# A two-block transformer kernel on one core: the opening turns x's first tile as it is loaded, and the position distances move to GpSimd

## What is computed

```python
h = rms_norm(x, norm_mix_pre[i])          # x * rsqrt(mean(x*x) + eps) * gain
z = h @ w_in[i]                           # (256 x 1024) @ (1024 x columns)
c_q, c_kv, k_rope, q_c, k_c, v_c, g_a, g_b, g_c = jnp.split(z, split_points, axis=-1)
...
dist = jnp.abs(pq[..., :, None] - pw[..., None, :]).astype(jnp.float32)
s = s - slopes[None, None, :, :, None, None] * dist[:, :, None, None]
```

## Time and profile before

| what | value |
|---|---|
| time, median of 3 runs | 1905.62 us (1905.6 to 1906.89) |
| profiled execution, its span from first to last instruction | 1904.2 us (the profile gives no other time of it) |
| TensorE busy | 1868.7 us, 98% of the span |
| VectorE, ScalarE, GpSimd busy | 1107.1, 958.9, 150.4 us |
| first product of TensorE starts | 13.03 us |
| moved from memory | 330.48 MB, 174 GB/s over the span |

### The profile page before, as it was taken

The page is one execution under the profiler, slowest core; times in us unless marked ns, Lnnn a source line. Parts: engine busy times, 40 slices in busy tenths (PEclk is TensorE's granted clock), DMA queues, the critical chain, the costliest instruction groups (busy, mean ns, idle before and its releaser), DMA issues.

```text
span 1904.2 us, 26150 instructions
## 1 busy us (share of the span) xinstructions
PE 1868.7 (98%) x8988; PEld 1523.3 (80%) x8988; DVE 1107.1 (58%) x1365; ACT 958.9 (50%) x1277; POOL 150.4 (8%) x259
## 2 busy tenths in 40 slices
PE   8999999999999999999999999999999999999998
PEld 7777888887877888888788887788888888868887
DVE  6666565448676575446754456655465445575454
ACT  5664454445675464445544446644454444564443
POOL 5210010001300010000100012000011000100000
PEclk9999999999999999999999999999999999999999
DMA  6335565554524546565655554455565564526553
GB/s 225 123 119 184 179 217 190 178 183 151 166 90 166 205 164 204 193 198 177 201 190 178 179 202 141 143 195 179 182 219 170 184 198 169 195 90 197 178 178 107
DMA packets 204987, 332.72 MB, mean 175 GB/s; under 512 B 11360, under 2 KB 150240, under 8 KB 204896
## 3 DMA queue, kind: packets, MB, share of 16 engines
q1 hardware_dynamic: 200240, 319.08, 49.9%
q0 software_dynamic: 3120, 11.02, 1.7%
q10 hardware_dynamic: 1536, 1.47, 0.2%
HBM read 330.48 MB, written 1.05 MB: 174 GB/s over the span
## 4 chain that ended last, share of the span: by engine, by line
PE 88%; issue 4%; DVE 3%; ACT 3%; DMA 1%; POOL 0%; DVEq 0%; SPq 0%; POOLq 0%; ACTq 0%
PE ps L571 27%; PE ps L565 27%; PE ps L556 27%; PE ps L598 3%; ACT whi L1254 1%; PE ps L771 1%; PE ps L759 1%; PE ps L787 1%; ACT prob L1352 1%; DVE wlo L1738 1%; DMA raw<-w_in_dram 0%; DVE prob L1878 0%; DMA xs<-x_dram 0%; DVE prob L1851 0%; DVE act_lo L1744 0%
## 5 line engine op out<-in xcount | busy, mean ns | idle before, releaser
L1738 DVE TENSOR_TENSOR wlo<-raw,whi 128x2048 fp32r<-128x2048 f32 (+1 forms) x306 | 690.6, 2257 | 510.3 <-ACT whi L1254 509.8
L1254 ACT ACTIVATE whi<-raw 128x2048 fp32r<-128x2048 f32 (+1 forms) x306 | 576.9, 1885 | 422.4 <-PE ps L565 422.3
L571 PE MATMUL ps<-whi,act_hi 128*128 128x512 f32 (+2 forms) x1632 | 442.0, 392 | 5.1 <-issue 2.4
L556 PE MATMUL ps<-wlo,act_hi 128*128 128x512 f32 (+2 forms) x1632 | 438.7, 387 | 0.0
L565 PE MATMUL ps<-whi,act_lo 128*128 128x512 f32 (+2 forms) x1632 | 432.2, 386 | 1.5 <-DVE act_lo L1744 1.5
L565 PEld LDWEIGHTS ps<-whi,act_lo 128*128 128x128 f32 x1632 | 303.9, 188 | 64.4 <-DVE act_lo L1744 2.3
L556 PEld LDWEIGHTS ps<-wlo,act_hi 128*128 128x128 f32 x1632 | 302.2, 188 | 61.8 <-issue 1.1
L571 PEld LDWEIGHTS ps<-whi,act_hi 128*128 128x128 f32 x1632 | 297.5, 188 | 64.1 <-issue 2.8
L1299 ACT ACTIVATE hid<-ps,stat 128x256 f32<-128x256 f32 x132 | 62.6, 474 | 282.9 <-PE ps L598 197.4
L2320 POOL TENSOR_TENSOR stat<-stat,eps 128x1 f32<-128x1 f32 x43 | 22.4, 521 | 1471.4 <-ACT prob L1286 1471.1
L1791 DVE SCALAR_TENSOR_TENSOR hid<-ps,stat,hid 128x256 f32<-128x256 f32 x132 | 63.6, 482 | 123.7 <-ACT hid L1299 123.7
(11 more groups left out here) (217 smaller groups left out, 1611.5 us busy)
## 6 DMA issues: line engine op xcount, KB each, us to landing
raw<-ffn_w_gate_dram SPq DMA_DIRECT2D x88, 512.0 KB, 4.0
raw<-ffn_w_up_dram SPq DMA_DIRECT2D x88, 512.0 KB, 5.0
raw<-ffn_w_down_dram SPq DMA_DIRECT2D x88, 512.0 KB, 3.9
raw<-w_in_dram SPq DMA_DIRECT2D x64, 512.0 KB, 4.4
raw<-w_ffn_gate_dram SPq DMA_DIRECT2D x44, 512.0 KB, 4.0
raw<-w_ffn_up_dram SPq DMA_DIRECT2D x44, 512.0 KB, 5.0
raw<-w_ffn_down_dram SPq DMA_DIRECT2D x44, 512.0 KB, 3.9
raw<-a_w_qkv_dram SPq DMA_DIRECT2D x24, 512.0 KB, 4.5
```

The lines of the kernel that those rows point to most:

```text
L556: last = nc.tensor.matmul(o, hi, a, start=False, stop=last_pass and stop and i == len(parts) - 1)
L571: nc.tensor.matmul(o, hi, a, start=start and i == 0, stop=False)
L1254: nc.scalar.activation(whi[:, u % SLOTS, 0:words], raw[:, u % SLOTS, 0:words], ACT.Copy)\
L1738: nc.vector.tensor_tensor(wlo[:, u % SLOTS, 0:words], raw[:, u % SLOTS, 0:words], whi[:, u % SLOTS, 0:words].bitcast(F32), ALU.subtract)\
```

## The change

Seven things are done, all of them in the first microseconds, apart from the last:

1. x's first tile is transposed as it is loaded (`xs` instead of `ht`). The gain comes as a column of 8 words for each partition (`first_col`, a new input of 4 KB), and VectorE multiplies it in on the way out of PSUM into `ht`; ScalarE and VectorE then take high and low parts from `ht`.
2. The gain's row is loaded once (4 KB, one partition) instead of to all partitions, and two TensorE products of a row of ones with it spread it over 128 partitions in PSUM (`first_row`), where VectorE reads it for x's second tile.
3. The 18 transposes of the identity are gone (WARM_START = 0).
4. x's second tile is issued ahead of the splits of unit 0; `posk` is issued between the splits of units 0 and 1, on a semaphore of its own, so that GpSimd's angles wait for `posq` and `freq` alone.
5. VectorE takes the low parts of x's second tile ahead of the position work.
6. Of the position work only the six steps that split positions stay on VectorE. The eight steps of distances are twelve on GpSimd, between the load of the next gains and `inverse(1)`.
7. TensorE's first four products of units 0 and 1 wait by halves of the unit (`first_hi`, `by_halves`), in each layer; ScalarE splits units 0 and 1 of each layer in two halves. The 42 start increments of semaphores are shared between TensorE and VectorE.

```diff
-WARM_SHORT, WARM_LONG, WARM_START = 6, 3, 18
+WARM_SHORT, WARM_LONG, WARM_START = 6, 3, 0
...
 # TensorE
                 for i, (outs, hi, lo, whs, wls) in enumerate(parts):
+                    if half is not None and 2 * i == len(parts):
+                        half()
...
                 if t == 0:
-                    if ready.seam:
+                    if by_halves:
+                        pe.wait_ge(sem("first_hi"), w.at("first_hi", u + 1))
+                    elif ready.seam:
                         unit_hi_there(u)
...
-            for s in counted:
+            for s in counted[0::2]:
                 pe.sem_inc(s, BASE)
             pe.wait_ge(s_ident, 2)
             w.layer = 0
-            rows(TN_MIX, "h_ready", 0)[1](0)
-            stay_warm(WARM_START)
+            pe.wait_ge(s_in["x0"], 16)
+            for g in range(2):
+                turn(TN_MIX + g, lambda j: xs[:, 0, (4 * g + j) * P:(4 * g + j + 1) * P], 4, bank=2 + g)
+            pe.wait_ge(s_in["gain"], 16)
+            for n in range(2):
+                last = nc.tensor.matmul(ps[:, n, :], one_row, first_gain[:, n * 512:(n + 1) * 512],
+                                        start=True, stop=True)
+            last.then_inc(s_row, 1)
...
 # ScalarE
+                    in_two = halves or (w.layer is not None and UNITS1 <= u < UNITS1 + 2)
...
-            act.dma_start(gains[:, 0, :], A["gains"][0:1, :].partition_broadcast(P).rearrange("p a n -> p (a n)"))\
-                .then_inc(s_in["gain"], 16)
-            act.dma_start(posk[:, :], A["positions"][0:1, :].partition_broadcast(P).rearrange("p a n -> p (a n)")).then_inc(s_in["pos"], 16)
+            act.dma_start(first_col[:, :], A["first_col"][:, :]).then_inc(s_col, 16)
+            act.dma_start(first_gain, A["gains"][0:1, :]).then_inc(s_in["gain"], 16)
...
-            turned_rows_hi(TN_MIX, (0,))
...
-            first_split(0)
+            for g, (there, n) in enumerate(((s_turned, 1), (sem("h_ready"), w.at("h_ready", 1)))):
+                act.wait_ge(there, n)
+                nc.scalar.activation(act_hi[:, 4 * g:4 * g + 4, 0:P],
+                                     ht[:, 0, g * 512:(g + 1) * 512].rearrange("p (j c) -> p j c", j=4),
+                                     ACT.Copy).then_inc(sem("turn_hi"), 1)
             act.dma_start(xs[:, 1, :], A["x"][0, P:S, :]).then_inc(s_in["x1"], 16)
-            first_split(1)
+
+            split(1, True)
+            act.dma_start(posk[:, :], A["positions"][0:1, :].partition_broadcast(P).rearrange("p a n -> p (a n)")).then_inc(s_posk, 16)
+            split(1, True)
...
 # VectorE
-            nc.vector.tensor_tensor(ht[:, 0, :], xs[:, 0, :], gains[:, 0, :], ALU.mult).then_inc(sem("h_ready"), 1)
-            turned_rows_lo(TN_MIX, 0)
...
+            first = [ht[:, 0, g * 512:(g + 1) * 512].rearrange("p (j c) -> p j c", j=4) for g in range(2)]
+            for g, done_part in enumerate((s_turned, sem("h_ready"))):
+                dve.wait_ge(sem("turn_done"), w.at("turn_done", TN_MIX + g + 1))
+                cols = first_col[:, 4 * g:4 * g + 4].unsqueeze(2).to_broadcast([P, 4, P])
+                nc.vector.tensor_tensor(first[g], ps[:, 2 + g, :].rearrange("p (j c) -> p j c", j=4), cols, ALU.mult)\
+                    .then_inc(done_part, 1)
...
-            nc.vector.tensor_tensor(ht[:, 1, :], xs[:, 1, :], gains[:, 0, :], ALU.mult).then_inc(sem("h_ready"), 1)
+            first_row = ps[:, 0:2, :].rearrange("p b n -> p (b n)")
+            nc.vector.tensor_tensor(ht[:, 1, :], xs[:, 1, :], first_row, ALU.mult).then_inc(sem("h_ready"), 1)
+            turned_rows_lo(TN_MIX, 1)
...
-            dve.wait_ge(s_parts, n_parts[0])
-            for t in range(T):
-                parts(nc.vector.tensor_scalar(mask[:, t, :], kf[:, 0, :], posf[:, 1, t:t + 1], 4096.0,
-                                              ALU.subtract, ALU.mult))
...
-            turned_rows_lo(TN_MIX, 1)
             split(1)
...
 # GpSimd
-            pool.wait_ge(s_in["pos"], 64)
+            pool.wait_ge(s_in["pos"], 48)
...
             load_gain(1, 1)
+            pool.wait_ge(s_parts, PART_STEPS)
+            for t in range(T):
+                parts(nc.gpsimd.tensor_scalar(mask[:, t, :], kf[:, 0, :], posf[:, 1, t:t + 1], 4096.0,
+                                              ALU.subtract, ALU.mult))
+                parts(nc.gpsimd.tensor_scalar(df[:, t, :], kf[:, 1, :], posf[:, 2, t:t + 1], None, ALU.subtract))
...
+                parts(nc.gpsimd.tensor_tensor(mask[:, t, :], mask[:, t, :], df[:, t, :], ALU.subtract))
+            pool.wait_ge(s_parts, n_parts[0])
             inverse(1)
-
-            pool.wait_ge(s_parts, DISTANCE_STEPS)
```

More of the change, by code:

```diff
@@ L57 @@
 ANGLE_STEPS = 25
-PART_STEPS, DISTANCE_STEPS = 6, 14
+PART_STEPS = 6
 F32 = mybir.dt.float32
@@ L366, in two_blocks @@
         s_end_result = sem("end_result")
+        s_posk = sem("posk_in")
+        s_col = sem("first_col_in")
+        s_row = sem("first_row")
+        s_turned = sem("first_turned")
+        one_row = hid[0:1, 1, 0:P]
+        first_gain = gains[0:1, 0, :]
         blk = ctx.enter_context(nc.Block())
@@ L545, in turn_hi_there, with product @@
                 pe.wait_ge(sem("turn_hi"), w.at("turn_hi", flags[:k + 1].count("1")))
-            def product(parts, start, stop, weights_lo=None, amid=None, rows_lo=None, rows_first=False):
+            def product(parts, start, stop, weights_lo=None, amid=None, rows_lo=None, rows_first=False, half=None):
                 def by_lo_weights(last_pass):
@@ L576, in product, with unit_product @@
                 return by_lo_rows(True)
-            def unit_product(u, t, kt, parts, start, stop, ready=None):
+            def unit_product(u, t, kt, parts, start, stop, ready=None, by_halves=False):
                 ready = ready or AT_ONCE
                 if t == 0:
-                    if ready.seam:
+                    if by_halves:
+                        pe.wait_ge(sem("first_hi"), w.at("first_hi", u + 1))
+                    elif ready.seam:
                         unit_hi_there(u)
@@ L589, in unit_product @@
                                weights_lo=(lambda: unit_there(u)) if t == 0 and ready.seam else None,
-                               amid=lambda i: ready.amid(t, kt + i), rows_lo=lambda: ready.rest(t, kt), rows_first=ready.rows_first and t == 0)
+                               amid=lambda i: ready.amid(t, kt + i), rows_lo=lambda: ready.rest(t, kt), rows_first=ready.rows_first and t == 0,
+                               half=(lambda: unit_hi_there(u)) if t == 0 and by_halves else None)
             def turn(k, src, n, rows=P, bank=None):
@@ L870, in layer1 @@
                                                   act_lo[:, 4 * j + k, t * P:(t + 1) * P], [vh[:, k, :]], [vl[:, k, :]])
-                                                 for k in range(4)], j == 0, j == 1, ready if c == 0 else None)
+                                                 for k in range(4)], j == 0, j == 1, ready if c == 0 else None,
+                                                by_halves=c == 0)
                             if t == T - 1 and j == 0:
@@ L1241, in _, with split @@
             done = [0]
-            def split(n):
+            def split(n, halves=False):
                 for _ in range(n):
@@ L2128, in _, with first_lo @@
             w.layer = 0
-            dve.wait_ge(s_in["gain"], 16)
-            dve.wait_ge(s_in["x0"], 16)
-            nc.vector.tensor_tensor(ht[:, 0, :], xs[:, 0, :], gains[:, 0, :], ALU.mult).then_inc(sem("h_ready"), 1)
-            turned_rows_lo(TN_MIX, 0)
-            for u in range(2):
-                for words, there, n in ((slice(0, UW // 2), s_first_hi, u + 1),
-                                        (slice(UW // 2, UW), sem("hi"), w.at("hi", u + 1))):
-                    dve.wait_ge(there, n)
+            for s in counted[1::2]:
+                dve.sem_inc(s, BASE)
+            dve.wait_ge(s_col, 16)
+            first = [ht[:, 0, g * 512:(g + 1) * 512].rearrange("p (j c) -> p j c", j=4) for g in range(2)]
[4 more added lines that the diff above has]
+                    .then_inc(done_part, 1)
+            for g in range(2):
+                hi_n[0] += 1
+                dve.wait_ge(sem("turn_hi"), w.at("turn_hi", hi_n[0]))
+                rest(act_lo[:, 4 * g:4 * g + 4, 0:P], first[g], act_hi[:, 4 * g:4 * g + 4, 0:P])\
+                    .then_inc(sem("turn_read_v"), 1)
+            def first_lo(u):
+                for words, there in ((slice(0, UW // 2), "first_hi"), (slice(UW // 2, UW), "hi")):
+                    dve.wait_ge(sem(there), w.at(there, u + 1))
                     last = nc.vector.tensor_tensor(wlo[:, u, words], raw[:, u, words],
```

52 lines of the change are left out of this document (32 added, 20 removed).

## The result

The changed kernel takes **1918.76 us** (median of 5 runs, 1917.26 to 1920.59) against 1905.6 for the kernel before in the same comparison: ratio 1.0066, 95% interval 1.0055 to 1.0077. That is 13 us slower. The forecast was 1908.2 with 1911.6 as its upper end: the sign was right, the size missed by 10.6 us.

The account below looks back on a forecast made before the run. TensorE, 98% busy, was taken as the bound, with GpSimd's chain to `inverse(1)` close under it. Delaying `z_half(0, 1)` from 31.14 to 34.0 put unit 5 at 42.2 against 39.59: 1905.62 + 2.6 = 1908.2 us, range 1904.0 to 1911.6.

Parts of the forecast that it names:

- Change = start of `z_half(0, 1)` - 31.14 - 0.27: Opening, VectorE to TensorE: total time moves with the start of `z_half(0, 1)`, forecast at 34.0, giving +2.6 us.
- so 6.25 stays: VectorE: from the start of `z_half(0, 1)` to unit 4's low part takes 6.25 us, as before.
- I take 0.40 for the eight one-input steps and 0.62 for the four others ... 6.1 us: GpSimd's twelve distance steps ahead of `inverse(1)`: 6.1 us with 0.4 of waits, bounds 4.4 to 7.4.
- The 0.04 given to steps slower than the bound: GpSimd's distance steps: a remaining chance of 0.04 that they are slower, for a change over +3.8 us.
- an estimate of 0.38 us for one input: GpSimd's distance steps: estimates from the skill page, 0.38 us for one input and 0.55 for two, 0.4 less in all.
- rival C: TensorE ahead of unit 4: the clock falls in the 5.5 us idle, +2.3 on top of 2.6, 1910.5; chance 0.22.
- the opening as running at the 1.2 GHz level: TensorE's opening: transposes 0.21 us apart early, 0.11 at 18.70, and a slow first product group, read as a low clock.
- Part 7 ... gains nothing: ScalarE's splits in each layer: cost 0.1 us of ScalarE and gain nothing at the loop's turn.
- It costs nothing as long as x's second tile is later: TensorE's opening: the first twelve products can take 5.1 us instead of 2.7, without cost while that tile comes later.
- the upper price: TensorE's opening: the two gain products were priced at 0.45 to 0.85 us each, ending by 7.6.
- The opening's 3.3 us for TensorE: TensorE reaches tile 1's low-row products at 20.0 and unit 4 at 34.7, 3.3 us gained, spent in the wait.

Follow-up runs that it names:

- e3: The kernel before with only the twelve distance steps moved to GpSimd ahead of `inverse(1)`: 1918.88 us against 1907.12, ratio 1.0062.
- e7: The changed kernel with the distances on GpSimd in seven steps over 128x512 instead of twelve over 128x256: 1918.48 us against 1907.33 for the kernel before.
- e9: The changed kernel with 80 transposes of the identity on TensorE ahead of unit 4 in each layer: 1926.54 us against 1906.92 for the kernel before.
- e4: The changed kernel with six of the twelve distance steps, absolute value left out: 1914.09 us against 1907.12 for the kernel before.
- e5: The kernel before with only 32 unused bytes of SBUF a partition added ahead of the blocks' tiles: 1909.29 us against 1907.33, ratio 1.0014.
- e6: The kernel before with only 40 unused bytes a partition, so the blocks' tiles start at multiples of 64 bytes: 1905.33 us against 1907.33, ratio 0.9993.
- e8: e1 with 8 bytes of padding and the gains' load moved from ahead of `inverse(1)` into the angle steps: 1905.07 us against 1907.33 for the kernel before.
- e1: The changed kernel with all position work back on VectorE, ahead of the low parts of x's second tile: 1906.97 us against 1907.12 for the kernel before.

## Why the prediction was wrong

**Right: the chain and its place.** "Change = start of `z_half(0, 1)` - 31.14 - 0.27" gives 38.44 - 31.14 - 0.27 = +7.03; unit 4's first product moved by 45.12 - 38.00 = +7.12. The two are this close by luck: the formula is for unit 5, and unit 4 had 0.34 us more to spare. What makes up for it is the term "so 6.25 stays": from `z_half(0, 1)` to the low part of unit 4 it was 43.71 + 1.35 - 38.44 = 6.62 us. With the gains there, VectorE's `scaled` multiplications run between the last inverses, and two of these took longer than the 0.55 us of the earlier trace rows. The sign and the engine were read correctly from the earlier trace rows, and e3 shows that this part by itself costs as much as the whole change. Unit 4's 7.12, the clock's 1.6 and the 0.4 just named are the opening's 9.15.

**The step that failed: "I take 0.40 for the eight one-input steps and 0.62 for the four others ... 6.1 us", with 7.4 as the upper bound.** Measured in the changed kernel: 11.9 us. The four steps with a scalar per partition took 1.15 and 0.93 (one held to 2.11), the four with a constant 0.83 each, the four two-input ones 0.71 each. The error was to take a copy of 128x256 (0.41) for any one-input step. The row of a two-input step (0.737) was the nearer in kind, since it does arithmetic; even that for all twelve, 9.2 with the waits, would have been 2.7 us short, 1.0 of it the held step. With the measured 11.9 the prediction's own sum gives 34.0 + 5.8 = 39.8 for `z_half(0, 1)`, less 1.5 for angle steps that ended earlier (24.39, forecast 25.9): 38.3. The 0.04 given to steps slower than the bound was far too small for a price that no row showed. The Trainium skill (GPSIMD Engine Reference, "Elementwise — side-by-side cycle accounting") gives 1.8 cycles an element as the best case of a tight loop, from which the prediction had worked out an estimate of 0.38 us for one input. With 0.83 to 1.15 us none of these steps ran like it. The 2.6 cycles for two inputs fit better: an estimate of 0.55 us for 256 columns from that page, against 1.28 - 0.71 = 0.57 us for 256 more columns in e7.

**Right in kind, its weight mis-set: rival C.** The clock fell in the idle ahead of unit 4. It was priced at 2.3 us and cost 1.6 (e9). Since it follows from a long idle, it belonged into the sum as soon as the idle was forecast at 5.5 us: e4, with 5.86 us idle, had it too. The prediction also read the opening as running at the 1.2 GHz level. The distances of transposes and products say half rate, but the granted clock of the profile is 1.00 from 0 to 16 us in both traces, so that level is read off the distances alone. That transposes can keep the clock up is shown by e9; that the 18 had raised it is read from the one slow product alone.

**Missing: the tiles' place in SBUF.** "Part 7 ... gains nothing" and the column of gains were costed at nothing. e5 shows 1.6 to 2.0 us for 32 bytes. What remains of the 2.2 (0.1 at the turn, 2.47 against 2.38) was not taken apart. Part 7 was not tried by itself; the equal rest of e6 and e8 speaks against it.

**Smaller steps.** x's first tile came at 4.64 (4.2 forecast), `freq` at 9.71 (8.7 to 8.9), the first product at 10.33 (9.9), x's second tile was taken up at 15.44 (15.6), TensorE was at tile 1's low-row products at 21.08 (20.0), at the end of its stream at 35.75 (34.7). The 15.44 is a hit for another reason than the one given: the tile was issued at 7.36 and landed 7.3 us later, at 14.7, and VectorE came to it only after the low part of unit 1. "It costs nothing as long as x's second tile is later" was wrong, though without effect on the total: the gained tile was there at 16.65, but TensorE, at half rate until some 15 us, turned it at 17.79, and that is most of the 1.1 us at 21.08. The gain products were four of 0.86 us, twice the upper price; they ended at 10.30, just before the first product. The opening's 3.3 us for TensorE came out as 2.3 and, as forecast, bought nothing, being spent in the wait.

**What stays open.** The profiled execution explains 11.4 of the 13.2 us of the medians. Which steps are held can make the difference: in the traces of e4, e7 and e9 the angle steps ended 2.7 us later than in this one, the fastest of its five, and in e9 unit 4 came 1.8 us later for it. But no trace of the slower executions of the changed kernel was taken.

## What to carry to other kernels

An engine that is idle 92% of the time can still be the one that sets the time: before work is put on it, find the next thing that waits for it in program order, and put the new work behind that. Price a step that no row shows by rows of the same kind of operation, not only of the same size, and let the range hold twice the nearest row. After a change that adds even a few bytes of SBUF, compare the products' distance in stretches that the change doesn't touch: here a shifted tile cost more than the opening of e1 had won.

## What the runs showed of the hardware

- Float32 steps on GpSimd over 128x256: a subtraction with a scalar per partition 0.93 us, with a multiplication by a constant in the same step 1.15, max or min with a constant 0.83, two tensors 0.71, a copy 0.41. VectorE did the first kind in 0.34 to 0.38 us (in e1).
- Products of 512 columns on operands 56 bytes past a multiple of 64 last 395 ns in the median, 24 past 392, at a multiple 389 (`four_lo`; the places are by the sizes in the code).
- The granted clock fell in TensorE's idle stretches of 9.37, 5.86, 11.83 and 11.12 us (changed kernel, e4, e3, e7), and at the loop's turn (2.2 to 2.8 us idle) in some executions and not in others. In the changed kernel it came back 4.3 us after work began again. In e9, with transposes of the identity in the same stretch, it stayed at 1.00.
- The granted clock is 1.00 from 0 to 16 us in both traces, and yet TensorE's work there comes at half rate at first. In the kernel before, TensorE ran at full rate within the first group of products, behind transposes from 7.56 to 13.03. In the changed kernel it was busy without a long gap from 4.64, with transposes to 6.58 and then 3.78 us of products of one row, and four full products still took 1.91 us at 12.21, against 1.07 later. That products of one row did not raise the clock is argued from this, not shown.
